# Both decay loads of the next group ahead of the token blocks on GpSimd's queue in a hybrid SSD block

## What is computed

```
hn = rmsnorm(h, norm_mix_w)
z, xbc, dt_raw, u, g_a, g_b = split(hn @ w_in)
y_a = mamba2_mixer(z, xbc, dt_raw, ...)   # conv, SSD scan, group norm, @ w_proj
y_b = s5_mixer(u, ...)                    # complex diagonal scan, gelu, @ w_glu
h = h + (sigmoid(g_a) * y_a + sigmoid(g_b) * y_b) @ w_out
h = h + conv_glu_ffn(rmsnorm(h, norm_ffn_w))
out = rmsnorm(h, norm_final_w)
```

```
decay[l, s] = exp(sum of a*dt over s < t <= l), for s <= l, else 0
y_head[l] = sum over s of (C[l] . B[s]) * decay[l, s] * dt[s] * x_head[s]
```

## Time and profile before

| | |
|---|---|
| Median of three executions | 1676.27 us |
| The profiled execution, its own time | 1676.26 us |
| Its span, first to last instruction | 1674.5 us |
| TensorE matmul busy | 1662.4 us (99%) |
| VectorE busy | 1319.5 us (79%) |
| ScalarE busy | 980.1 us (59%) |
| GpSimd busy | 234.2 us (14%) |
| Mean granted TensorE clock | 0.998 of full speed |
| HBM rate over the span | 213 GB/s |

### The profile page before, as it was taken

The page is one execution under the profiler, slowest core; times in us unless marked ns, Lnnn a source line. Parts: engine busy times, 40 slices in busy tenths (PEclk is TensorE's granted clock), DMA queues, the critical chain, the costliest instruction groups (busy, mean ns, idle before and its releaser), DMA issues.

```text
span 1674.5 us, 24301 instructions
## 1 busy us (share of the span) xinstructions
PE 1662.4 (99%) x8292; PEld 1389.1 (83%) x8292; DVE 1319.5 (79%) x1685; ACT 980.1 (59%) x1353; POOL 234.2 (14%) x340
## 2 busy tenths in 40 slices
PE   9999999999999999999999999999999999999997
PEld 8888888888788888888888888888888888888886
DVE  8999999999999986545766858888878888845555
ACT  7676676666587877444547754444444444454553
POOL 7843342221001110000000200000000000000001
PEclk9999999999999999999999999999999999999999
DMA  7666666666767676556786577777777777655653
GB/s 255 214 198 197 204 206 199 193 190 184 240 232 274 212 253 203 197 191 206 241 253 227 179 230 240 239 242 245 243 241 242 244 240 243 223 199 190 194 185 124
DMA packets 177641, 364.78 MB, mean 218 GB/s; under 512 B 17520, under 2 KB 41632, under 8 KB 177440
## 3 DMA queue, kind: packets, MB, share of 16 engines
q1 hardware_dynamic: 163968, 339.84, 62.3%
q0 software_dynamic: 12880, 23.09, 5.4%
q10 hardware_dynamic: 720, 0.93, 0.2%
HBM read 338.55 MB, written 18.95 MB: 213 GB/s over the span
## 4 chain that ended last, share of the span: by engine, by line
PE 65%; DVE 6%; ACT 2%; DMA 1%; issue 1%; DVEq 0%; ACTq 0%
PE psum L1955 20%; PE psum L1957 20%; PE psum L1956 20%; PE psum L1916 3%; DVE wlo L1204 2%; PE psum L1918 2%; DMA raw<-in_w_gate 1%; DVE dec L1550 1%; ACT whi L734 1%; DVE dec L1556 1%; ACT xtok L943 0%; DVE vn L1882 0%; PE psum L2045 0%; DVE xblk L1473 0%; ACT dec L936 0%
## 5 line engine op out<-in xcount | busy, mean ns | idle before, releaser
L1204 DVE TENSOR_TENSOR wlo<-raw,whi 128x1024 fp32r<-128x1024 f32 x580 | 709.0, 1229 | 309.2 <-ACT whi L734 302.5
L734 ACT ACTIVATE whi<-raw 128x1024 fp32r<-128x1024 f32 x580 | 612.4, 1058 | 579.9 <-PE psum L1957 447.7
L1916 PE MATMUL psum<-act,whi 128*128 128x512 f32 x1088 | 342.5, 396 | 0.0
L1955 PE MATMUL psum<-whi,nw 128*128 128x512 f32 x704 | 274.1, 389 | 0.0
L1957 PE MATMUL psum<-whi,nw 128*128 128x512 f32 x704 | 273.9, 389 | 0.0
L1956 PE MATMUL psum<-wlo,nw 128*128 128x512 f32 x704 | 273.9, 389 | 0.0
L1918 PEld LDWEIGHTS psum<-act,wlo 128*128 128x128 f32 x1088 | 204.4, 188 | 48.3
L1918 PE MATMUL psum<-act,wlo 128*128 128x256 f32 x1088 | 213.7, 278 | 0.0
L1916 PEld LDWEIGHTS psum<-act,whi 128*128 128x128 f32 x1088 | 165.6, 189 | 3.3 <-issue 3.2
L1955 PEld LDWEIGHTS psum<-whi,nw 128*128 128x128 f32 x704 | 132.1, 188 | 27.5
L1956 PEld LDWEIGHTS psum<-wlo,nw 128*128 128x128 f32 x704 | 132.1, 188 | 27.4
(11 more groups left out here) (262 smaller groups left out, 2325.4 us busy)
## 6 DMA issues: line engine op xcount, KB each, us to landing
raw<-in_w_up SPq DMA_DIRECT2D x176, 512.0 KB, 4.8
raw<-in_w_zx SPq DMA_DIRECT2D x96, 512.0 KB, 3.8
raw<-in_w_down SPq DMA_DIRECT2D x88, 512.0 KB, 3.7
raw<-in_w_gate SPq DMA_DIRECT2D x64, 512.0 KB, 5.7
raw<-in_w_proj SPq DMA_DIRECT2D x48, 512.0 KB, 4.4
raw<-in_w_bc SPq DMA_DIRECT2D x32, 512.0 KB, 3.8
raw<-in_w_glu SPq DMA_DIRECT2D x32, 512.0 KB, 4.4
raw<-in_w_out SPq DMA_DIRECT2D x32, 512.0 KB, 4.5
```

Source lines behind the costliest of these rows:

```text
L734: fn(whi[:, s, :], raw[:, s, :], ACTF.Copy).then_inc(hi_ready, 1)
L1204: V.tensor_tensor(wlo[:, s, :], raw[:, s, :], whi[:, s, :], ALU.subtract).then_inc(lo_ready, 1)
L1916: mm(psum[:, b + t, :], whi[:, s, cols(t)], x, start=first, stop=False)
L1955: mm(banks[:, t, :], x_hi, high[:, k], start=j == 0 and k == 0, stop=False)
```

## The change

In each of the seven turns of GpSimd's loop the two waits for the heads and the two decay loads come first, and the write and the fetch of x's blocks follow. Nothing is added or removed: the same DMAs, waits and buffers, in another order on this one queue.

```diff
             for i in range(GROUPS - 1):
+                pool.wait_ge(y_ready, i * 2 + 1)
+                load_decay(i + 1, 0)
+                pool.wait_ge(y_ready, i * 2 + 2)
+                load_decay(i + 1, 1)
                 if i:
                     token_write(i + 1)
-                pool.wait_ge(y_ready, i * 2 + 1)
-                load_decay(i + 1, 0)
-                if i:
                     token_fetch(i + 1)
-                pool.wait_ge(y_ready, i * 2 + 2)
-                load_decay(i + 1, 1)
```

## The result

The changed kernel took 1680.54 us, the median of 9 runs (1679.24 to 1683.19), against 1676.27 us for the kernel before (9 runs). The ratio is 1.0025, with a 95% interval from 1.0016 to 1.0034: 4.3 us slower, a small loss that is clear of noise, where the prediction had 0.3 us gained. The time lies inside the stated range, but it moved the other way than forecast.

A forecast was written before the change was run, and what follows sets the result against it. The prediction took TensorE as the bound, with a floor of 25.24 us a turn, and VectorE as second. From 1676.26 us it took 0.5 gained and gave 0.2 back: 1676.0 us, range 1674.4 to 1681.

The forecast's parts named there:

- the one on weights: Weight loads beside the two decay loads: ScalarE's waits move to mid-turn, costing TensorE nothing; 1 us per turn if cover failed.
- Rival C: Weights starved by the burst of decay loads: 6 turns by 1 us, 1682 us; chance 0.05.
- B: Fetch lands after H+21.2 (H: turn's first heads matmul), `xtok` starts late, TensorE waits before heads: 1681 to 1687 us; chance 0.17.
- The gain term: VectorE's three scan waits for decay rows, 3.7 us, go; TensorE gains 0.5 us, bounds 0 and about 2.
- The bound of 0: Lower bound of the gain from removing VectorE's scan waits: TensorE gains nothing.
- The sum of landings: GpSimd's queue, from a turn's first heads matmul H: loads issued H+1.8 and H+3.2, writes land H+13.4, fetch H+20.1.
- The last harmless start: Latest start of ScalarE's `xtok` that costs TensorE nothing at the next heads: H+21.2, H being the turn's first heads matmul.
- The range: Whole-kernel time of 1674.4 to 1681 us, taking in the main forecast and the late-fetch rival's nearer half.
- rival B's nearer half: Late fetch reaching half way to its bound: 0.8 us a turn, 5 us in all, 1681 us.
- The chance of 0.16 for slower: Chance that the whole kernel measures slower by more than about 0.2%, 3.35 us; same had 0.82, faster 0.02.

The follow-up runs named there:

- e2: Changed kernel with the four writes put ahead of both decay loads and the fetch last: 1685.05 us, 1.0045 of the kernel before.
- e4: Kernel before plus a 576 KB copy between DRAM tensors behind the first decay load in turns 1 to 6: 1687.12 us, ratio 1.0060.
- e8: Kernel before with the first decay load moved ahead of the write in turns 5 and 6 alone: 1676.21 us, ratio 0.9997.
- e5: Kernel before reordered: first decay load, writes, second load once they landed, fetch held until four TensorE units after the heads (three in turn 1): 1676.56 us.
- e6: As e5, with the fetch held for one more TensorE unit: 1678.97 us, 1.0015 of the kernel before.
- e3: Changed kernel with the writes put between the two decay loads and the fetch last: 1678.34 us, 1.0009 of the kernel before.

## Why the prediction was wrong

**The step that failed** is the one on weights: "ScalarE's waits for weights should move from the end of a turn to its middle, at no cost to TensorE: it is covered by the lead of up to four units." The lead covers TensorE's own units; its wait for a low part stayed small (1.2 us on the weight loads, 0.7 before). It does not cover the heads. The heads need `xtok`, the exponentials and the blocks, which stand in ScalarE's and VectorE's in-order queues behind the high and low parts of the late units. The slack there was 3.2 us in turn 1 and 0.7 us in turn 4 before (the table above); the units came 4.7 and 2.0 us later than before, and the difference, 1.5 and 1.3 us, went to TensorE. In turns 2 and 5, whose stretches grew by 0.5 and 0.7 us, the way is not shown so plainly. Rival C was this burst, but I looked only for a wait of TensorE for `wlo`, gave it a chance of 0.05 and 1 us in each turn. Its cause was right, its way and its sign that would show it were not; the sign that did come, weight loads of the heads waiting for the blocks, I had put down to B. e2 and e4 show the cause: they lose most, with the weights late and the fetch inside its bound.

**The gain term** was 0.5 us, from scans that wait for decay rows. The waits went as said, 3.7 us to none, but in the changed kernel TensorE gained at most the 0.3 us of the last stretch. e8 shows that these waits alone are worth nothing that can be measured here. The bound of 0 was nearest.

**The sum of landings** was half right. The decay loads were issued at H+1.8 in all six turns, and at H+2.5 to H+4.2 for the second, about as told. The writes landed at H+11.3 to H+13.4 where I had H+13.4, with bounds of 10.1 and 16.4; before they landed at H+7.0 to H+11.9. Their place behind the decay loads did delay them: the last write took 5.7 to 8.7 us to land in the changed kernel, and 4.5 to 5.8 us in e2, which issues the same six DMAs together with the writes in front. The fetch landed at H+17.7 to H+18.9, at least 1.2 us ahead of my H+20.1, since the writes came up to 2.1 us sooner than I had them and it then took 4.1 to 6.4 us, against 5.8 to 7.0 before.

**Rival B**, the late fetch, fell. It had over three times C's chance because the order of the landings was in plain sight in the earlier trace rows, and each transfer in the chain had a row. Who else used the DMA engines in these 10 us had one short paragraph and no row with the landing of a weight load. The last harmless start, H+21.2, held to about 1 us (e5, e6).

**The range** held the time by luck: rival B's nearer half happened to cover it, and B's mechanism was not at work. The chance of 0.16 for slower was too low for a change that puts 1536 KB at once beside a weight stream for which ScalarE already waited 25.9 us.

What stays open is why the units land earlier in e3 than in the changed kernel with the same bytes in flight (its later second decay load is the likely reason, not tested), and how VectorE and ScalarE share the loss in turns 2 and 5; no run takes these apart.

## What to carry to other kernels

When a change moves DMAs closer together, ask first what else is in flight in that window and who takes it up next, in order; only then who waits for the DMAs that were moved. A prefetch lead protects the consumer of the prefetched pieces: other work that stands behind them in a helper's queue has only the slack of that queue, here 3.2 us in one turn and 0.7 us in another. Find that bound from the trace (the landing after which the helper works without a gap) before you move a DMA. An engine's wait for data can be removed without any gain if the engine has spare time in that turn, so weigh a wait by what the next engine does, not by its length.

## What the runs showed of the hardware

Weight loads of 512 KB took 4.5 and 5.6 us to land beside the old order and 6.7 and 10.1 us beside two decay loads and four writes issued together on GpSimd's queue, in the same turn. From H+7.5 to H+12.5, while the second decay load and the writes were in flight in the changed kernel, the DMA engines were full in both. So GpSimd's transfers and SyncE's share the engines, and a load of one queue took up to 1.8 times as long for what the other queue had in flight. The Trainium skill says in "DMA: Bandwidth & Descriptors", section "Issuing engines are not separate DMA queues", that DMAs of different issuing engines run on the same DMA engines and interleave; the numbers agree. The two views of those 5 us, turn 1 of before and of the changed kernel:

```profile
484.10:489.10 5.00, 5.00 (x24) 4.14 (x23) 4.93 (x9) 2.44 (x4) 0.92 (x2) 1.00 1.04 399
```

```profile
484.90:489.90 5.00, 5.00 (x24) 4.15 (x23) 4.93 (x9) 1.91 (x2) 0.00 (x0) 1.00 1.02 383
```

I had not expected how much the landing time of one and the same fetch varies with the rest of the traffic. Its 384 KB took 3.3 to 3.5 us in four turns of e6, with a DMA share of 0.59 to 0.64 over the fetch and three weight units in flight during it; 6.4 us beside a decay load, share 1.03; and also 6.4 us in turn 2 of the changed kernel, where no decay load was in flight any more, but five weight units were, share 0.97.
